# Norm stages of a macaron layer rewritten: squares beside the products, roots by Ln and Exp, the next stage following by tiles

## The reference

```python
def rmsnorm(x, g):
    y = xf * lax.rsqrt(jnp.mean(xf * xf, axis=-1, keepdims=True) + RMS_EPS)
    return (y * g).astype(x.dtype)
def pre(x, mod, i, g):
    return rmsnorm(x, g) * (1.0 + mod[3 * i + 1]) + mod[3 * i]
def post(x, y, mod, i, g, res_w):
    return x + res_w * mod[3 * i + 2] * rmsnorm(y, g)
def swiglu(h, w_gate, w_up, w_down):
    return (jax.nn.silu(h @ w_gate) * (h @ w_up)) @ w_down
...
x = post(x, swiglu(pre(x, mod_l, 0, ...), w1_gate, w1_up, w1_down), mod_l, 0, g_post[l, 0], 0.5)
# the same for ctx; then the mixer between pre(.., 1, ..) and post(.., 1, .., 1.0)
x = post(x, swiglu(pre(x, mod_l, 2, ...), w2_gate, w2_up, w2_down), mod_l, 2, g_post[l, 2], 0.5)
```

## Time and profile before

| | |
|---|---|
| median of 3 runs | 3304.87 us (3301.5 to 3307.31) |
| the profiled execution | 3300.94 us |
| its span, first to last instruction | 3299.1 us |
| PE matmul, busy | 3104.7 us (94%) |
| DVE, ACT busy | 1810.7 us (55%), 1030.7 us (31%) |
| mean granted TensorE clock | 0.976 |

### The profile page before, as it was taken

The page is one execution under the profiler, slowest core; times in us unless marked ns, Lnnn a source line. Parts: engine busy times, 40 slices in busy tenths (PEclk is TensorE's granted clock), DMA queues, the critical chain, the costliest instruction groups (busy, mean ns, idle before and its releaser), DMA issues. The chain is left out here.

```text
span 3299.1 us, 50736 instructions
## 1 busy us (share of the span) xinstructions
PE 3104.7 (94%) x21174; PEld 2665.1 (81%) x21174; DVE 1810.7 (55%) x2184; ACT 1030.7 (31%) x1298; POOL 11.9 (0%) x18
## 2 busy tenths in 40 slices
PE   6899999999999999999599998999888999999997
PEld 3588878878887787887378897777768999999996
DVE  3346556555565565655644645665346555555554
ACT  3222122122222212212532452222355444444433
POOL 0000000000000000000000000000000000000000
PEclk9999999999999999999899999999898999999998
DMA  9735445444464665755123440000434555555551
GB/s 322 270 108 184 153 141 185 141 159 140 153 204 164 219 229 184 274 203 192 67 78 101 134 150 12 2 2 2 155 112 141 178 179 181 182 174 180 184 179 64
DMA packets 323470, 501.73 MB, mean 152 GB/s; under 512 B 7964, under 2 KB 244004, under 8 KB 307716
## 3 DMA queue, kind: packets, MB, share of 16 engines
q1 hardware_dynamic: 321792, 494.73, 44.5%
q0 software_dynamic: 704, 4.62, 0.4%
q10 hardware_dynamic: 836, 0.33, 0.0%
HBM read 497.55 MB, written 2.10 MB: 151 GB/s over the span
## 5 line engine op out<-in xcount | busy, mean ns | idle before, releaser
L1800 PE MATMUL ps<-xn,parts 128*128 128x256 f32 (+1 forms) x11184 | 1900.9, 332 | 59.3 <-DVE xn L1413 50.3
L1800 PEld LDWEIGHTS ps<-xn,parts 128*128 128x128 f32 x11184 | 1693.2, 191 | 268.3 <-DVE xn L1413 32.3
L1199 DVE TENSOR_TENSOR parts<-raw,parts 128x1024 fp32r<-128x1024 f32 x642 | 768.9, 1221 | 571.0 <-ACT parts L650 570.5
L650 ACT ACTIVATE parts<-raw 128x1024 fp32r<-128x1024 f32 x640 | 664.9, 1055 | 1189.4 <-PE ps L1800 967.7
L1800 PE MATMUL ps<-h_parts,parts 128*128 128x512 f32 (+1 forms) x4224 | 742.2, 337 | 26.7 <-DVE h_f L1255 25.2
L1800 PEld LDWEIGHTS ps<-h_parts,parts 128*128 128x128 f32 x4224 | 648.5, 190 | 120.5 <-issue 35.9
L1276 DVE TENSOR_TENSOR acc<-acc,ps 128x256 f32<-128x256 f32 (+1 forms) x336 | 184.2, 548 | 308.7 <-PE ps L1800 308.5
L1219 DVE SCALAR_TENSOR_TENSOR macc<-raw,cs,macc 128x2048 f32<-128x2048 f32 x150 | 348.1, 2345 | 0.0
L1255 DVE TENSOR_TENSOR h_f<-silu_g,ps 128x512 f32<-128x512 f32 (+1 forms) x42 | 39.5, 942 | 223.9 <-PE ps L1800 223.9
L660 ACT ACTIVATE h_parts<-h_f 128x512 fp32r<-128x512 f32 (+1 forms) x42 | 35.1, 836 | 333.2 <-DVE h_f L1255 333.2
L1800 PE MATMUL ps<-sq_buf,c 128*128 128x256 f32 (+1 forms) x160 | 64.1, 518 | 17.2 <-ACT sq_buf L773 12.5
(11 more groups left out here) (199 smaller groups left out, 1252.3 us busy)
## 6 DMA issues: line engine op xcount, KB each, us to landing
raw<-in_w_mod SPq DMA_DIRECT2D x144, 1024.0 KB, 6.3
raw<-in_w_gate SPq DMA_DIRECT2D x88, 1024.0 KB, 5.1
raw<-in_w_up SPq DMA_DIRECT2D x88, 1024.0 KB, 5.1
raw<-in_w_down SPq DMA_DIRECT2D x88, 1024.0 KB, 5.1
raw<-in_w_in SPq DMA_DIRECT2D x41, 1024.0 KB, 5.3
raw<-in_w_out SPq DMA_DIRECT2D x16, 1024.0 KB, 5.5
x_in<-in_ctx SPq DMA_DIRECT2D x2, 1024.0 KB, 6.7
x_in<-in_x SPq DMA_DIRECT2D x2, 1024.0 KB, 12.0
```

What stands on the lines that cost most here:

```text
L650: nc.scalar.activation(parts[:, unit % PART_SLOTS, 0, :], raw[:, slot, b * UNIT:(b + 1) * UNIT], ACT.Copy).then_inc(hi_ready, 1)
L1199: nc.vector.tensor_tensor(parts[:, pslot, 1, :], raw[:, slot, b * UNIT:(b + 1) * UNIT], parts[:, pslot, 0, :].bitcast(F32), ALU.subtract)\
L1800: return nc.tensor.matmul(o, lhsT, rhs, start=start, stop=stop)
```

## The change

**Down products.** In all rounds but the very first, the first down unit no longer waits for `h_ok` of the second half of h.

**Step 1.** The squares of the last products of an FFN are taken between the weight splits of its last round, four tiles behind each group j, and PE sums them behind the next group; in the output projection ACT squares out of PSUM as it evicts a pair. The buffers wk are four. One item is 512 columns: one tile, or behind the mixer two tiles.

**Step 2.** The root is exp(-ln(mean + eps) / 2), both on ACT, with a request for the table set that holds both, behind the wait for the sums.

**Step 3.** ACT multiplies by post_g (`gate`), DVE by rb and adds; ACT squares three items later. The copy of x goes by DMA from the POOL queue; of the second stream none is made, and FFN 2 adds up in a buffer acc3 that POOL clears.

**Step 4.** DVE multiplies by rb, ACT scales and shifts in one instruction per 256 columns and rounds, DVE makes the rest. The four units of the next products wait for four tiles each, not for all 16.

**End.** The output is transposed, copied and stored in four column quarters.

```diff
-            for t in range(2):
-                sp.wait_ge(out_copied, 4 * (t + 1))
-                sp.dma_start(out[0, t * P:(t + 1) * P, :], out_rows[:, t, :]).then_inc(out_sem, 16)
-            sp.wait_ge(out_sem, 32)
+            for q in range(4):
+                sp.wait_ge(out_copied, 2 * (q + 1))
+                sp.dma_start(out[0].rearrange("(t p) n -> p t n", p=P)[:, :, 512 * q:512 * q + 512],
+                             out_rows[:, :, 512 * q:512 * q + 512]).then_inc(out_sem, 16)
+            sp.wait_ge(out_sem, 64)
...
-            pool.wait_ge(units_done, PART_SLOTS + 2 * S_KV.weight)
+            pool.wait_ge(units_done, PART_SLOTS + 2 * S_KV.weight - 8)
             for t in range(4):
                 src = (ctx if t < 2 else x)[0, (t % 2) * P:(t % 2 + 1) * P, :]
                 pool.dma_start(x_again[:, t, :], src).then_inc(x_re, 16)
 
+            for q in range(4):
+                pool.wait_ge(x_ok, 4 * q + 4)
+                pool.dma_start(x1[:, 4 * q:4 * q + 4, :], acc[:, 4 * q:4 * q + 4, CTX:TOK]).then_inc(kept, 16)
...
+            pool.wait_ge(hs["vt_mm"], HEADS * PER["vt_mm"])
+            nc.gpsimd.memset(acc3[:], 0.0).then_inc(acc3_zero, 1)
...
+            def squares(r, n, a):
+
+                if n >= 4:
+                    act.wait_ge(sq_used, n - 3)
+                n0 = SQ_AT[r][0] if n < (SQ_AT[r][1] or 99) else SQ_AT[r][1]
+                nc.scalar.activation(slot_of(n, r), span(a, r, n - n0), ACT.Square).then_inc(sq_ok, 1)
...
+                    if sums is not None and u >= 19 and u % 2:
+                        r, a = sums
+                        j = (u - 19) // 2
+                        if j == 0:
+                            act.wait_ge(h_split, 2 * (G + 1))
+                        last_squares(r, a, G, j)
+                if sums is not None:
+                    last_squares(sums[0], sums[1], G, 3)
+
+            def last_squares(r, a, G, j):
+
+                per = 4 if r == 0 else 2
+                for e in range(per):
+                    n = per * j + e
+                    act.wait_ge(down_added, 1 + 16 * G + (n + 1) * (4 // per))
+                    squares(r, SQ_AT[r][0] + n, a)
...
+            def inv_root(n, N, total):
+
+                act.wait_ge(sq_used, total)
+                if n == 2:
+                    act.wait_ge(const_ok, 2)
+                nc.scalar.preload_act_table_set("natural_log_exp_and_others")
+                nc.scalar.activation(rb[:, 0:N], ps[:, 7, 0:N], ACT.Ln, scale=1.0 / D, bias=eps_b).then_inc(ln_ok, 1)
+                act.wait_ge(ln_ok, n - 1)
+                nc.scalar.activation(rb[:, 0:N], rb[:, 0:N], ACT.Exp, scale=-0.5).then_inc(rb_ok, 1)
...
+            def gate(r, n, a):
+
+                k0, k1 = items(r)[n]
+                for k in range(k0, k1):
+                    for s in range(1 if r else 0, 2):
+                        c0 = 0 if r else s * CTX
+                        nc.scalar.activation(a[:, k, c0:c0 + SEQ], a[:, k, c0:c0 + SEQ], ACT.Copy,
+                                             scale=post_g[:, s, k:k + 1]).then_inc(gated, 1)
+
+            def post(r, N, a):
+
+                inv_root(2 + 2 * r, N, SQ_AT[r][0] + len(items(r)))
+                act.wait_ge(coef_ok, (4, 6, 7)[r])
+                num = len(items(r))
+                for n in range(num + 3):
+                    if n < num:
+                        gate(r, n, a)
+                    if n >= 3:
+                        act.wait_ge(x_ok, X_AT[r] + n - 2)
+                        squares(r, SQ_AT[r][1] + n - 3, a)
+
...
+                def hi(n):
+                    act.wait_ge(v_ok, V_AT[r] + 2 * (n + 1))
+                    nc.scalar.activation(span(dst[:, 0], r, n), slot_of(n, r), ACT.Copy).then_inc(v_hi, 1)
+                for n in range(num):
+                    act.wait_ge(scaled, SC_AT[r] + n + 1)
+                    for h in range(2):
+                        k, s = (n, h) if r == 0 else (2 * n + h, 1)
+                        c0 = SEQ * h
+                        nc.scalar.activation(wk[:, n % 4, c0:c0 + SEQ], wk[:, n % 4, c0:c0 + SEQ], ACT.Identity,
+                                             scale=pre_a[:, s, k:k + 1], bias=modT[:, row, s, k:k + 1]).then_inc(v_ok, 1)
+                    if n:
+                        hi(n - 1)
+                hi(num - 1)
```

The DVE side, PE's sums, and the waits of the next products:

```diff
+            def post(r, a, resid):
+
+                num = len(items(r))
+                dve.wait_ge(rb_ok, 2 + 2 * r)
+
+                def add(n):
                     if resid is None:
-                        dve.wait_ge(xT_ok, KT + k + 1)
-                        src = ps[:, k % 4, :]
...
+                        dve.wait_ge(xT_ok, KT + n + 1)
+                    dve.wait_ge(y_scaled, DONE_AT[r] + n + 1)
+                    src = ps[:, n % 4, :] if resid is None else span(resid, r, n)
+                    nc.vector.tensor_tensor(span(a, r, n), span(a, r, n), src, ALU.add).then_inc(x_ok, 1)
+                for n in range(num):
+                    dve.wait_ge(gated, GATED_AT[r] + 2 * (n + 1))
+                    nc.vector.tensor_tensor(span(a, r, n), span(a, r, n), rb_of(r), ALU.mult).then_inc(y_scaled, 1)
+                    if n:
+                        add(n - 1)
+                add(num - 1)
...
+                def lo(n):
+                    dve.wait_ge(v_hi, VH_AT[r] + n + 1)
+                    nc.vector.tensor_tensor(span(dst[:, 1], r, n), slot_of(n, r),
+                                            span(dst[:, 0], r, n).bitcast(F32), ALU.subtract).then_inc(xn_ok, 1)
+                for n in range(num):
+                    if n >= 4:
+                        dve.wait_ge(xn_ok, XN_AT[r] + n - 3)
+                    nc.vector.tensor_tensor(slot_of(n, r), span(a, r, n), rb_of(r), ALU.mult).then_inc(scaled, 1)
+                    if n >= 2:
+                        lo(n - 2)
+                lo(num - 2)
+                lo(num - 1)
...
-                    pe.wait_ge(h_ok, 2 * G + 3)
+                    if first:
+                        pe.wait_ge(h_ok, 2 * G + 3)
                     pe.wait_ge(silu_ok, 2 * G + 2)
...
+            def sums(r, n, N):
+
+                n0, n1 = SQ_AT[r][0], SQ_AT[r][1] or 99
+                base = n0 if n < n1 else n1
+                e, num = n - base, len(items(r))
+                pe.wait_ge(sq_ok, n + 1)
+                if r == 0:
+                    last = mm(ps[:, 7, :], ones, wk[:, n % 4, :], e == 0, e == num - 1)
+                else:
+                    mm(ps[:, 7, 0:SEQ], ones, wk[:, n % 4, 0:SEQ], e == 0, False)
+                    last = mm(ps[:, 7, 0:SEQ], ones, wk[:, n % 4, SEQ:2 * SEQ], False, e == num - 1)
+                last.then_inc(sq_used, 1)
...
+                        if follow is not None and j < 2:
+                            pe.wait_ge(xn_ok, follow + 2 * (2 * j + b + 1))
                         wide_unit(seg, i, j0 + j, b, banks, N, a)
...
+                    if last_of is not None and j:
+                        if j == 1 and row is not None:
+                            pe.wait_ge(mod_copied, row + 7)
+                        per = 4 if last_of == 0 else 2
+                        for e in range(per):
+                            sums(last_of, SQ_AT[last_of][0] + per * (j - 1) + e, N)
                     if j == 0 and row is not None:
                         mod_reduce(seg, i, row, both)
                     if j == 2 and row is not None:
                         transpose_mod(row)
+                if last_of is not None:
+                    per = 4 if last_of == 0 else 2
+                    for e in range(per):
+                        sums(last_of, SQ_AT[last_of][0] + 3 * per + e, N)
...
+            for k in range(KT + 4):
+
+                if k < KT:
+                    if k >= 4:
+                        pe.wait_ge(x_ok, k - 3)
+                    for t in range(4):
+                        last = nc.tensor.transpose(ps[:, k % 4, P * t:P * t + P], x_again[:, t, P * k:P * k + P], ident)
+                    last.then_inc(xT_ok, 1)
...
+                    if k == 4:
                         pe.wait_ge(rb_ok, 2)
-                    pe.wait_ge(sq_ok, KT + k - 1)
...
+                    sums(0, KT + k - 4, TOK)
...
                 for uu in range(4):
+                    if n == 0:
+                        pe.wait_ge(xn_ok, KT + 4 * (uu + 1))
                     wide_unit(seg, i, 2 * pr + uu // 2, uu % 2, (bank, bank + 1), N, a)
```

More of the change, by code:

```diff
@@ L748, in _ @@
                     ffn_round(S_A1, i, 2 * i + 1 + half, TOK, h_parts, i + 2 if half else None, j0=12 * half)
-            with act.Fori(0, S_A2.iters) as i:
+            with act.Fori(0, S_A2.iters - 1) as i:
                 ffn_round(S_A2, i, i + 7, TOK, h_parts, i + 5)
[L752 to L764, removed]
@@ L788, in in_pairs @@
-            def in_pairs(seg, i, N, dst, tile, done):
-                ubase = PART_SLOTS + 2 * seg.weight + 8 * i
-                for u in range(8):
```

(35 more changed lines are left out.)

218 lines of the change are left out of this document (86 added, 132 removed).

## The result

The changed kernel takes 3231.39 us (median of 4 runs, 3230.52 to 3235.97) against 3304.0 of before (3301.5 to 3307.31): a ratio of 0.978, 95% interval 0.977 to 0.980. That is 72.6 us less. The profiled executions, 3300.94 and 3231.15 us, differ by 69.8 us, their spans by 69.7.

A forecast was written before the change was run, and what follows sets the result against it. Products on PE bound the rounds, with a pause each round; three norm stages hand tiles between engines. Savings of 25.2 + 19.7 + 13.5 + 5.4 = 63.8 us against 3304.87 gave 3241 us, range 3230 to 3260.

The forecast's parts named there:

- Down products: FFN rounds: removing PE's wait for the DVE multiply of h saves the whole recorded pause, 14.8 + 10.4 = 25.2 us.
- Step 1: Squares and sums in the norm stages: PE still pays every sum; 13.9 us in A, 7.1 in B and C.
- Step 2: Roots in the norm stages: table load, Ln and Exp on the path, 2.7 us, or 2.3 for 256 columns.
- Step 3: Post part of the norm stages: ACT becomes the busiest, 1.34 to 1.56 us an item; 24 us in A, 12.3 in B.
- Step 4: Pre part and following products: two of four units hidden; third unit's start 27.4 us in A, 16.6 in B, then remaining products.
- B: Norm stage behind the output projection, to the end of four units: 60.9 us before, 47.4 predicted, saving 13.5.
- A: Norm stage behind FFN 1, to the end of the next block's first four units: 103.3 us before, 83.6 predicted, saving 19.7.
- C: Norm stage at the kernel's end, from the last product on: 36.6 us before, 31.2 predicted, saving 5.4.
- rival 1: FFN rounds: the pause moves to the second down unit, taking back 10 to 25 us, 3251 to 3266; chance 0.08.
- Rival 3: Roots: table loads cost twice the row, a drain behind each of five, 6.4 us more, 3247; chance 0.05.
- a load of the active set is free: Roots: reloading an already active table set might cost nothing, so for three of five roots 3.8 us less.
- Rival 4: Ahead of the projections: waiting for x's DMA copy makes the kernel slower; at 110 us landing, 3323 us; chance 0.02.

The follow-up runs named there:

- run 1: Kernel before with one edit: the first down unit no longer waits for h_ok of the second half, except in the first round; 3271.99 us, ratio 0.990.
- run 2: Changed kernel with the wait for h_ok of the second half put back in all rounds; 3263.91 us, ratio 0.988.
- Run 4: Changed kernel with the last products' squares and sums of both FFNs placed behind the round's loop instead of between its units; 3231.96 us, ratio 0.978.
- run 7: Changed kernel with squares written as fp32r and summed with fp32r ones in one pass; 3209.45 us, ratio 0.972.
- Run 9: Changed kernel with the five roots of before: DVE scales and takes the reciprocal, ACT takes Sqrt; 3240.24 us, ratio 0.981.
- run 5: Changed kernel with the table load asked for ahead of an FFN's last squares and nowhere else; 3225.77 us, ratio 0.976.
- run 10: Changed kernel with the multiply by post_g back on DVE, in one instruction with rb; 3230.42 us, ratio 0.978.
- run 6: Changed kernel with the third and fourth unit split early, behind FFN 1's last squares and inside the post stage behind the output projection; 3219.57 us, ratio 0.975.
- run 3: Changed kernel, but the first four units behind the pre stages wait for all of xn instead of following by tiles; 3245.21 us, ratio 0.982.
- run 11: Changed kernel with two wk buffers instead of four in the pre stages, DVE making rest n - 2 ahead of multiply n; 3265.15 us, ratio 0.988.

## Why the prediction was right, point by point

The total came out 6 us too small by errors of both signs: the rounds 5.6 us too little, B 2.4 too much, A and C 0.3 and 0.6 too little, and 1.7 us between the stages that the change does not explain. That it lies within the range at all is in part luck: had B come out as predicted, the time would have been 3229.

- **Down products: mis-sized, 25.2 us against 31.** The mechanism held: no pause at the second down unit (rival 1 did not come), and the splits behind kept up. The step that failed is "the removed wait is the whole pause": I priced it at the idle time that the waits record, 1.48 and 0.94 us. By the spacing of the multiplies a pause cost 1.78 and 1.18, and runs 1 and 2 confirm the sum. The other 0.3 and 0.24 us do not show as idle time. In FFN 2 of before, the chain of work has from one pause's end to the next 70.32 us, of which 576 products are recorded as 69.38 us busy, and without pauses a round takes (714.2 - 714.2 / 31) / 10 = 69.1 us (the 714.2 us are ten and a third rounds). So the difference lies in what is recorded as busy; why is open. This term is most of the 6 us between the predicted and the measured gain.

```profile
2676.75 69.38 PE ps L1800 x576
...
2747.07 69.38 PE ps L1800 x576
```

- **Step 1: right in size (A 13.8, B and C 7.1 and 7.2), and so was its reason.** Run 4 shows that moving squares between the splits gives nothing, since PE pays each sum; run 7 shows that shortening the sums gave 17 us in step 1 (8.5 + 4.6 + 4.3).
- **Step 2: right, 2.7 and 2.2 us a root.** Run 9 gives 9 us for all five. Rival 3 fell (run 5), and so did the bound that a load of the active set is free.
- **Step 3: right for A, mis-sized for B.** In A 24.0 us against 24, taken between 22.9 for ACT alone and 24.9 with PE's slow start, and both parts show. ACT's items came 1.32 us apart (1.34 predicted). PE's second sum stood 2.10 us behind its square (1583.54 and 1581.44), the twelfth still 1.89 (1596.51 and 1594.62), and the last sum ended at 1600.97, 2.35 us behind the end of the last square: at 1.30 us an item PE could not catch up. Run 7 takes this lag away, 1.5 us. But the saving is not the move of the multiply from DVE to ACT: run 10 shows that it bought nothing. In B I had ACT again, 12.3 us, and it took 2423.91 - 2409.84 = 14.1: at a granted clock of 0.71 a sum of two tiles held PE 10.10 / 8 = 1.26 us, and the first could begin only 4 us behind the root. I had charged slow products in A and forgotten them in B.
- **Step 4: right, 27.2 us against 27.4 in A and 16.6 in B as predicted** (root to third unit), at 1.50 us an item where I had 1.52. The idle time ahead of the third unit came out at 4.98 and 2.80 us, for 5 and 3, and its cause is the split (run 6). Following by tiles is worth 14 us (run 3). The two units in B took 7.5 us, not 6.8, at the clock of 0.71.
- **C: right, 30.6 us against 31.2.** Root 2.1 us (2.3), the last transposes end 17.5 us behind it (17.6), the tail is 3.8 us (4.2).
- **Rival 4, the wait for the copy of x:** the four copies landed in 3.3 us (median), and no wait for them shows.
- **Open.** Runs 1, 3, 4, 9 and 10 give 31 + 14 + 1 + 9 - 1 = 54 of the 72 us. The rest (post in the new order with ACT's copies gone, scale and shift in one instruction with the four buffers that run 11 halves, the end in quarters) was not taken apart.

## What to carry to other kernels

Price a pause by the spacing of a repeated event, not by the idle time that the waits record: here each cost a quarter of a microsecond more. Before moving work beside the engine that binds, ask whether that engine still pays for it; here the squares moved for nothing, and shortening the sums gave 22 us, at the price of rounded squares. And when a consumer follows its producer by tiles, prepare the rest of its input too: two pauses of 5 and 3 us ahead of the third unit cost 12 us in all, in part because the products behind them ran at a lower clock.

## What the runs showed of the hardware

A DVE reciprocal of 128x512 fp32 took 3.35 us, of 256 columns 1.76, five times a multiply of the same size (0.69). A table load took 1.28 us whether its set was already active or not, and no drain showed beside it (1.30 us from the instruction ahead to the one behind). A sum over partitions of 512 fp32 columns held PE 0.86 us, and 17 us went from 32 such items when they became fp32r (run 7, step 1). Short idle stretches of PE lowered its clock: 1.00 granted just ahead of pauses of 5.0 and 2.8 us, 0.87 and 0.71 in the stretches behind them, 1.00 in the same units without them (run 6).
